# A fused two-block transformer kernel: GpSimd subtracts the low parts of nine down-projection weight tiles in each FFN of block 2

## The chip, the cores and the metric

The kernel runs on one core of a Trainium2 chip. The metric is the device time of one launch in microseconds (us), the median of several launches. Beside it stands one profiled execution, from which all durations below are read.

The engines are named as the profile names them: PE (TensorE, matrix multiply), PEld (its weight load), DVE (VectorE), ACT (ScalarE), POOL (GpSimd), SP (SyncE, which here only issues DMAs). SBUF is the on-chip memory that all of them read, PSUM the accumulators that PE writes.

## The reference, cut to what matters

The reference applies two transformer blocks to 256 tokens of width 1024, each block with two layers. The change touches the feed-forward part of block 2, `conv_ffn`, in both layers:

```
u = x @ w_up                                  # 1024 -> 5632
u = causal depthwise convolution of 3 taps over the tokens, plus bias
a, g = split(u, 2)                            # 2816 each
f = (a * silu(g)) @ w_down                    # 2816 -> 1024
x = layer_norm(DEEPNORM_ALPHA * x + f)
```

Everything is float32.

## The kernel before, in words

**Split weights.** PE multiplies in a rounded format (float32r). To keep float32 accuracy each weight tile is held in two parts. ACT copies the loaded tile `raw` into `whi` (rounded), line 1335. DVE then forms the remainder `wlo = raw - whi`, line 1714, one TENSOR_TENSOR with both operands in SBUF. PE multiplies with both parts. A tile is 128 partitions by 2048 elements (1 MB). "hi(t)" and "lo(t)" below are these two steps for tile t, and "the split" of a tile on DVE is lo(t).

**Order of the tiles.** `plan_tiles` writes out the order in which PE uses them. The FFN of a layer has 11 steps (FS = 11). Step s uses g_s (gate half of w_up, 256 features), u_s (up half), and then one tile of w_down: d_{s-1} for s = 1 to 5, none in step 6, d_{s-2} for s = 7 to 10. After step 10 come d_9 and d_10 together. So there are 33 tiles to each FFN.

**Buffers.** `raw` and `wlo` are rings of five tiles, `whi` is a ring of three. One more set (`xraw`, `ext`) holds g_0 of an FFN, and the first tile of the next layer's w_in. hi(t) can be made once PE is done with the tile three places earlier (`hi_room`). `serve(key)`, on ACT and on DVE, makes every split whose room comes free with tile `key`; both engines make all splits in the same written order (`split_order`). Each engine runs its instructions strictly in program order.

**One step s of the FFN of block 2.**
- PE: 32 matmuls for g_s, 32 for u_s (`by_features_wide`, lines 809 to 813) and 24 for the down tile (`down`, lines 737 to 739). It waits for lo of the tile (`take`), for the sums of the step before, and for `hid_ready` of the hidden slice that the down tile multiplies.
- ACT: copies the low half of the gate sums out of PSUM (L1397), runs the convolution's middle tap (L1686), hi(g_{s+1}) (L1335), silu (L1693). Then the same for the up half: L1397, L1686, hi(u_{s+1}), and last the hi of the next down tile, d_s in steps 1 to 4 and d_{s-1} in steps 7 to 9.
- DVE: adds the halves of the gate sums (L1877, one operand in PSUM), two more taps in four SCALAR_TENSOR_TENSORs (L2319), lo(g_{s+1}). Then L1877 and L2319 for the up half, the product (L2335), its rounded part (L2341), its remainder (L2343, which raises `hid_ready`), then lo(u_{s+1}), then lo of the same down tile as ACT.
- POOL: nothing. In block 2 it computes the reciprocal square roots of the norms (`norm_scale`, L2370), some copies (L2424, L2430) and the softmax division of the attention (L2382). Its next instruction in an FFN is the one for the norm behind it.

Down tiles 9 and 10 are split by DVE during step 10 and behind it. In step 9 of the first layer's FFN the split of the next layer's first w_in tile (into `ext`) stands ahead of lo(g_10).

Of the kernel before, what the change touches and what calls it, by code (L numbers as in the profile page):

```python
# [8 lines left out]
F32 = mybir.dt.float32  # L9
F32R = mybir.dt.float32r  # L10
I32 = mybir.dt.int32
ALU = mybir.AluOpType
# [8 lines left out]
L = 2  # L21
TC = 256
FF = 2816
FS = FF // TC
# [201 lines left out]
def build(nc, w, c, out):  # L226
    tiles, ti, geo = plan_tiles(w)
# [12 lines left out]
    split_order = []  # L240
    split_ring = [i for i in ring if i not in between.values()]
    split_seq = {i: q for q, i in enumerate(split_ring)}
    for i in halved:
        here = [e for e in extra if extra[e] == i]
        split_order += here + [i] if here and tiles[here[0]][0][1] == "in" else [i] + here
    rank = {i: q for q, i in enumerate(split_order)}
    load_order = []
    for i in order:
        load_order += [e for e in extra if extra[e] == i and tiles[e][0][1] == "in"]
# [26 lines left out]
    def unit0(block, l):  # L276
        return next(u for u, x in enumerate(units) if x[0] == block and x[1] == l)

    with ExitStack() as ctx:
# [3 lines left out]
        def sem(name):  # L283
            return ctx.enter_context(nc.semaphore(name))
# [77 lines left out]
        mem_ready = sem("mem_ready")  # L362
        hi_ready = sem("hi_ready")
        lo_ready = sem("lo_ready")
        tile_done = sem("tile_done")
        ident_loaded = sem("ident_loaded")
        angles_loaded = sem("angles_loaded")
# [159 lines left out]
        def tile_flat(buf, i):  # L527
            ap = tiles[i][1]
            return place(buf, i)[:, 0:ap.shape[1] * ap.shape[2]]

        def tile_view(buf, i):
            return tile_flat(buf, i).rearrange("p (k c) -> p k c", k=tiles[i][1].shape[1])
# [18 lines left out]
        def bc(ap, n):  # L551

            return ap.unsqueeze(1).broadcast_to([P, n, ap.shape[1]])
# [175 lines left out]
        def _(pe):  # L729
            def take(key):  # L730

                pe.wait_ge(lo_ready, rank[ti[key]] + 1)
                return tile_view("hi", ti[key]), tile_view("lo", ti[key])

            def product(o, lh, ll, rh, rl, first, last):
# [16 lines left out]
            def token_stage(block, name, l, n, ready, head, tail, free=lambda g, t: None, before={}):  # L752

                for q, t in passes(n, head, tail):
                    if (q, t) in before:
                        before[(q, t)]()
                    key = (block, name, l, q)
                    g, k0, whole = geo[key]
                    wh, wl = take(key)
                    kt, cols = wh.shape[1], wh.shape[2]  # L760
                    if k0 == 0:
                        free(g, t)
                    tok = slice(t * P, (t + 1) * P)
                    for kk in range(kt):
                        k = k0 + kk
                        turns_ready(ready, t, k)
                        ins = product(token_bank(g, t)[:, 0:cols], xhi[:, k, tok], xlo[:, k, tok], wh[:, kk, :],
                                      wl[:, kk, :], k == 0, k == KD - 1)
                    if t == 1:
                        ins.then_inc(tile_done, 1)  # L770
                    elif whole:
                        ins.then_inc(part_done, 1)

            def latent_products(key, outs, ah, al):

                wh, wl = take(key)
                kt = wh.shape[1]
                for t in range(NT):
                    for k in range(kt):
                        tok = slice(t * P, (t + 1) * P)  # L780
                        ins = product(outs[t], ah[:, k, tok], al[:, k, tok], wh[:, k, :], wl[:, k, :],
                                      k == 0, k == kt - 1)
                ins.then_inc(tile_done, 1)
# [327 lines left out]
            for l in range(L):  # L1111
# [78 lines left out]
                for i in range(2):  # L1190
                    pe.wait_ge(cmp_x, 2 * l + i + 1)
                    key = (2, "w1", l, i)
# [514 lines left out]
        def _(dve):  # L1707
# [2 lines left out]

            def split(i):

                dve.wait_ge(hi_ready, rank[i] + 1)
                v.tensor_tensor(tile_flat("lo", i), tile_flat("raw", i), tile_flat("hi", i).bitcast(F32),  # L1714
                                ALU.subtract).then_inc(lo_ready, 1)
# [643 lines left out]
        @block.gpsimd  # L2359
        def _(pool):  # L2360
            g = nc.gpsimd

            scaled = [0]

            def norm_scale(token_tiles=range(NT)):

                for t in token_tiles:
                    scaled[0] += 1
                    pool.wait_ge(ln_var, scaled[0])
                    g.tensor_tensor(rstd[:, t:t + 1], vare[:, t:t + 1], mhalf[:, t:t + 1],  # L2370
                                    ALU.pow).then_inc(ln_rstd, 1)

            def attention(block, l):
                first = 2 * unit0(block, l)
                count = 2 * sum(1 for x in units if x[0] == block and x[1] == l)
                for i in range(first, first + count):
                    u, hf = divmod(i, 2)
                    nk = (units[u][3] + 1) * P
                    x = soft[:, u % 2].rearrange("p (a q) k -> p a q k", a=2)[:, :, 2 * hf:2 * hf + 2, 0:nk]
                    rd = rden[:, u % 2, :].rearrange("p (a q) -> p a q", a=2)[:, :, 2 * hf:2 * hf + 2]  # L2380
                    pool.wait_ge(rden_ready, i + 1)
                    g.tensor_tensor(x, x, rd.unsqueeze(3).broadcast_to([P, 2, 2, nk]),  # L2382
                                    ALU.mult).then_inc(prob_ready, 1)

            pool.wait_ge(mhalf_ready, 1)
            norm_scale()
            norm_scale()
            pool.wait_ge(tables_ready, 1)
            for l in range(L):
                pool.wait_ge(ki_var, l + 1)  # L2390
                g.tensor_tensor(rstd[:, 0:NT], vare[:, 0:NT], mhalf[:, 0:NT], ALU.pow).then_inc(ki_rstd, 1)

                t1 = pt[:, 1:3, :].rearrange("p a b -> p (a b)")[:, 0:640].rearrange("p (h d) -> p h d", h=10)
                t2 = pt[:, 2:4, :].rearrange("p a b -> p (a b)")[:, 384:1024].rearrange("p (h d) -> p h d", h=10)
                x = proj1[:, 0, QA:QA + 640].rearrange("p (h d) -> p h d", h=10)
                for h0, h1 in ((0, H), (H, H + 2)):

                    pool.wait_ge(proj_ready, 8 * l + (5 if h0 == 0 else 7))
                    n, hs = h1 - h0, slice(h0, h1)
                    g.tensor_tensor(t1[:, hs], x[:, hs], bc(cos64[:, 0, :], n), ALU.mult)  # L2400
                    g.tensor_tensor(t2[:, hs, 0:32], x[:, hs, 32:64], bc(sin64[:, 0, 0:32], n), ALU.mult)
                    g.tensor_tensor(t2[:, hs, 32:64], x[:, hs, 0:32], bc(sin64[:, 0, 32:64], n), ALU.mult)
                    pool.drain()
                    if h0 == 0:
                        g.tensor_tensor(roped[:, 0, 0:4 * P].rearrange("p (r a d) -> p a r d", a=2, d=DH),
                                        t1[:, 0:8, :].rearrange("p (a r) d -> p a r d", a=2),
                                        t2[:, 0:8, :].rearrange("p (a r) d -> p a r d", a=2), ALU.add)
                    else:
                        g.tensor_tensor(roped[:, 0, 4 * P:5 * P].rearrange("p (h d) -> p h d", h=2),
                                        t1[:, 8:10, :], t2[:, 8:10, :], ALU.add).then_inc(qka_roped[0], 1)  # L2410
                attention(1, l)
                norm_scale()

                for t in range(NT):
                    for _ in range(2 if l == L - 1 else 1):
                        norm_scale([t])

            for l in range(L):
                pool.wait_ge(c_var, l + 1)
                g.tensor_tensor(rstdc[:], varc[:], mhalf[:], ALU.pow).then_inc(c_rstd, 1)  # L2420

                pool.wait_ge(proj2_ready, 8 * l + 6)
                for t in range(NT):
                    ins = g.tensor_copy(nqp[:, t, :].rearrange("p (r g d) -> p g r d", r=4, g=2),  # L2424
                                        proj2[:, t, NQ:NQ + 512].rearrange("p (g r d) -> p g r d", g=2, r=4))
                ins.then_inc(kd_ready, 1)

                pool.wait_ge(proj2_ready, 8 * l + 6)
                for e in range(2):
                    ins = g.tensor_copy(kdup[:, :, :, e, :],  # L2430
                                        proj2[:, :, KC:KC + 256].rearrange("p t (q d) -> p t q d", q=4))
                ins.then_inc(kd_ready, 1)
                attention(2, l)
                for _ in range(3):
                    norm_scale()


_NAMES = [
# [26 lines left out]
```

## Time and profile before

| | us |
|---|---|
| median of 3 launches | 1569.63 (1567.81 to 1573.33) |
| the profiled execution's own time | 1568.68 |
| its span | 1566.4 |
| PE busy | 1503.0 (96%) |
| DVE busy | 1072.9 (68%) |
| ACT busy | 765.3 (49%) |
| POOL busy | 122.9 (8%) |

The mean granted TensorE clock was 0.986 of full speed. PE is busy nearly all the time; what an edit beside it can change is the idle time between its matmuls. The chain of waits, which follows the last instruction back to what released it at each step, is 75% PE and 14% DVE. The FFN of the first layer of block 2 lies at about 940 to 1127 us of the span, that of the second at about 1373 to 1557 us.

### The profile page before, as it was taken

To read this page: it belongs to the slowest core of one execution; us is meant where nothing else is said; L and a number is where in the kernel's file an instruction comes from. 1 tells how busy PE (TensorE), PEld (TensorE's weight loads), DVE (VectorE), ACT (ScalarE), POOL (GpSimd) and SP (SyncE) were. 2 spreads that over 40 slices of the span, in tenths; PEclk is the share of its full clock that TensorE was granted. 3 is DMA by queue.
4 is the path that set the end of the run, shared out by engine and by line. 5 is a ranking of instruction groups with operands and counts; after the bars stand their busy time and mean duration, and the time that the engine had idled before them with its cause. 6 is when DMAs were issued, how large, how long until landed. Compare 5 with 4: busy or idle time off the path is not lost.

```text
span 1566.4 us, 21696 instructions
## 1 busy us (share of the span) xinstructions
PE 1503.0 (96%) x8429; PEld 1271.9 (81%) x8429; DVE 1072.9 (68%) x1735; ACT 765.3 (49%) x1136; POOL 122.9 (8%) x98
## 2 busy tenths in 40 slices
PE   8989999999899999999999999999899999999997
PEld 5767888888777888878877988888788779888886
DVE  7777687667766786685346457878852555678887
ACT  4563544444554444424474335555445653456562
POOL 0130000001210000011031000000010320000000
PEclk9999999999999999999899999999998999999999
DMA  7533655655236655635425635556545147345551
GB/s 259 193 104 132 217 190 191 213 190 181 90 119 209 218 189 189 242 114 168 154 91 172 218 114 188 188 188 215 162 123 172 62 151 246 130 162 188 189 187 55
DMA packets 184140, 265.01 MB, mean 169 GB/s; under 512 B 7336, under 2 KB 139366, under 8 KB 183912
## 3 DMA queue, kind: packets, MB, share of 16 engines
q1 hardware_dynamic: 178712, 258.38, 49.6%
q10 hardware_dynamic: 5328, 5.26, 1.0%
q8 instruction: 67, 1.10, 0.3%
q14 instruction: 33, 0.27, 0.1%
HBM read 258.38 MB, written 5.24 MB: 168 GB/s over the span
## 4 chain that ended last, share of the span: by engine, by line
PE 75%; DVE 14%; ACT 4%; issue 3%; DVEq 2%; POOL 1%; ACTq 0%; DMA 0%; POOLq 0%; SPq 0%
PE psw L810 16%; PE psw L737 7%; PE psw L739 7%; PE psw L738 7%; PE psw L809 7%; DVE wlo L1714 5%; PE psa L737 4%; PE psa L739 4%; PE psa L738 4%; PE psa L869 3%; PE psa L871 3%; PE psa L918 2%; PE psw L893 2%; PE psw L1196 1%; DVE r L2319 1%
## 5 line engine op out<-in xcount | busy, mean ns | idle before, releaser
L1714 DVE TENSOR_TENSOR wlo<-raw,whi 128x2048 fp32r<-128x2048 f32 (+3 forms) x199 | 448.5, 2264 | 125.4 <-ACT whi L1335 125.0
L810 PE MATMUL psw<-xboth,whi 128*128 128x512 f32 x1344 | 465.3, 396 | 4.8 <-DVE wlo L1714 4.8
L1335 ACT ACTIVATE whi<-raw 128x2048 fp32r<-128x2048 f32 (+3 forms) x199 | 374.2, 1886 | 180.2 <-PE psw L739 91.4
L809 PE MATMUL psw<-xboth,wlo 128*128 128x256 f32 x1176 | 327.9, 279 | 0.0
L810 PEld LDWEIGHTS psw<-xboth,whi 128*128 128x128 f32 x1344 | 242.9, 188 | 53.2 <-DVE wlo L1714 6.4
L809 PEld LDWEIGHTS psw<-xboth,wlo 128*128 128x128 f32 x1176 | 221.7, 189 | 7.5
L737 PE MATMUL psw<-whi,xboth 128*128 128x512 f32 (+3 forms) x472 | 181.8, 385 | 6.4 <-DVE wlo L1714 5.3
L739 PE MATMUL psw<-whi,xboth 128*128 128x512 f32 (+3 forms) x472 | 178.8, 379 | 0.0
L738 PE MATMUL psw<-wlo,xboth 128*128 128x512 f32 (+3 forms) x472 | 178.7, 379 | 0.0
L1397 ACT ACTIVATE r<-psw 128x512 f32<-128x512 f32 x88 | 52.6, 598 | 193.3 <-PE psw L810 182.8
L737 PE MATMUL psa<-whi,rr 128*128 128x512 f32 x352 | 137.3, 390 | 3.1 <-DVE wlo L1714 3.1
L738 PE MATMUL psa<-wlo,rr 128*128 128x512 f32 x352 | 137.0, 389 | 0.0
L2370 POOL TENSOR_TENSOR rstd<-vare,mhalf 128x1 f32<-128x1 f32 x26 | 36.7, 1414 | 1101.5 <-DVE vare L1736 1092.8
L2319 DVE SCALAR_TENSOR_TENSOR r<-r,pcol 128x254 f32<-128x254 f32 (+1 forms) x176 | 77.3, 481 | 57.1 <-ACT r L1686 53.8
L737 PEld LDWEIGHTS psw<-whi,xboth 128*128 128x128 f32 x472 | 88.8, 188 | 23.5 <-DVE wlo L1714 6.3
L739 PEld LDWEIGHTS psw<-whi,xboth 128*128 128x128 f32 x472 | 88.7, 188 | 15.8
L738 PEld LDWEIGHTS psw<-wlo,xboth 128*128 128x128 f32 x472 | 88.8, 188 | 15.0 <-issue 0.2
L739 PE MATMUL psa<-whi,rr 128*128 128x512 f32 x256 | 99.6, 389 | 0.0
L1877 DVE TENSOR_TENSOR r<-psw,r 128x512 f32<-128x512 f32 x88 | 60.5, 688 | 52.5 <-ACT r L1397 52.4
L1686 ACT ACTIVATE r<-r,pcol 128x256 f32<-128x256 f32 x88 | 48.2, 594 | 77.2 <-DVE r L1877 77.2
L1439 ACT ACTIVATE sy<-sy,nmx 128x256 f32<-128x256 f32 (+1 forms) x160 | 70.5, 444 | 20.9 <-DVE nmx L1813 20.9
L2382 POOL TENSOR_TENSOR sy<-sy,rden 128x512 f32<-128x512 f32 (+1 forms) x40 | 62.8, 1570 | 217.4 <-DVE rden L1825 176.1
(287 smaller groups left out, 2218.6 us busy)
## 6 DMA issues: line engine op xcount, KB each, us to landing
raw<-in_w_gu SPq DMA_DIRECT2D x44, 1024.0 KB, 5.1
raw<-in_ffn_w_up SPq DMA_DIRECT2D x42, 1024.0 KB, 5.1
raw<-in_w_down SPq DMA_DIRECT2D x22, 1024.0 KB, 4.9
raw<-in_ffn_w_down SPq DMA_DIRECT2D x22, 1024.0 KB, 4.9
raw<-in_w_in SPq DMA_DIRECT2D x20, 1024.0 KB, 5.3
raw<-in_xa_wkv SPq DMA_DIRECT2D x16, 1024.0 KB, 5.4
raw<-in_w_o SPq DMA_DIRECT2D x8, 1024.0 KB, 5.2
raw<-in_w_out SPq DMA_DIRECT2D x8, 1024.0 KB, 5.1
```

What stands on the lines that cost most here:

```text
L737: pe.matmul(o, lh, rh, start=first, stop=False)
L738: pe.matmul(o, lh, rl, start=False, stop=False)
L739: return pe.matmul(o, ll, rh, start=False, stop=last)
L809: pe.matmul(bank[:, 0:S], wl[:, k, cols], xhi[:, k, :], start=False, stop=False)
L810: ins = pe.matmul(bank.rearrange("p (i s) -> p i s", i=2), wh[:, k, cols], xboth[:, :, k, :], start=k == 0, stop=k == KD - 1)
L1335: nc.scalar.activation(tile_flat("hi", i), tile_flat("raw", i), ACT.Copy).then_inc(hi_ready, 1)
L1397: nc.scalar.activation(low_part[:, i], psw[:, 2 * i:2 * i + 2, S:2 * S], ACT.Copy).then_inc(low_out, 1)
L1439: ins = nc.scalar.activation(soft[:, u % 2, h, 0:nk], soft[:, u % 2, h, 0:nk], ACT.Exp, bias=nmx[:, u % 2, h:h + 1], scale=1.0, accum_out= ...
L1714: v.tensor_tensor(tile_flat("lo", i), tile_flat("raw", i), tile_flat("hi", i).bitcast(F32), ALU.subtract).then_inc(lo_ready, 1)
L1877: v.tensor_tensor((gsum, usum)[i].rearrange("p (c s) -> p c s", c=2), psw[:, 2 * i:2 * i + 2, 0:S], low_part[:, i], ALU.add).then_inc(ffn_ ...
L2319: ins = v.scalar_tensor_tensor(out=o, in0=whole[:, ch * S:(ch + 1) * S - lag], scalar=pcol[:, 1 + 2 * l, cc:cc + 1], in1=o, op0=ALU.mult, ...
L2382: g.tensor_tensor(x, x, rd.unsqueeze(3).broadcast_to([P, 2, 2, nk]), ALU.mult).then_inc(prob_ready, 1)
```

## The change

Nine down tiles of each FFN of block 2 (d_0 to d_8, in both layers: 18 tiles) are no longer split by DVE. POOL makes their lo with the same subtraction. It waits for hi of the tile and counts on a semaphore of its own, `pool_lo_ready`; the counts of `lo_ready` close up. POOL's loop stands between the second and the third norm of the layer.

```diff
+    pool_tiles = [ti[(2, "d", l, j)] for l in range(L) for j in range(FS - 2)]
+    pool_rank = {i: q for q, i in enumerate(pool_tiles)}
+    low_rank = {i: q for q, i in enumerate(i for i in split_order if i not in pool_rank)}
...
+        pool_lo_ready = sem("pool_lo_ready")
...
             def take(key):
 
-                pe.wait_ge(lo_ready, rank[ti[key]] + 1)
+                if ti[key] in pool_rank:
+                    pe.wait_ge(pool_lo_ready, pool_rank[ti[key]] + 1)
+                else:
+                    pe.wait_ge(lo_ready, low_rank[ti[key]] + 1)
                 return tile_view("hi", ti[key]), tile_view("lo", ti[key])
...
             def split(i):
 
+                if i in pool_rank:
+                    return
                 dve.wait_ge(hi_ready, rank[i] + 1)
                 v.tensor_tensor(tile_flat("lo", i), tile_flat("raw", i), tile_flat("hi", i).bitcast(F32),
                                 ALU.subtract).then_inc(lo_ready, 1)
...
                 attention(2, l)
-                for _ in range(3):
+                for _ in range(2):
                     norm_scale()
+                for j in range(FS - 2):
+                    down = ti[(2, "d", l, j)]
+                    pool.wait_ge(hi_ready, rank[down] + 1)
+                    g.tensor_tensor(tile_flat("lo", down), tile_flat("raw", down), tile_flat("hi", down).bitcast(F32),
+                                    ALU.subtract).then_inc(pool_lo_ready, 1)
+                norm_scale()
```

## Rows read from the trace of the kernel before

**Rows 1.** Waits inside FFN 1: engine, line, releaser, us in total, times, longest.

```profile
PE psw L810 <- DVE wlo L1714: 2.8, 3, 1.4
PE psa L737 <- DVE wlo L1714: 2.1, 1, 2.1
```

**Rows 2.** The same view inside FFN 2.

```profile
PE psw L810 <- DVE wlo L1714: 2.0, 2, 1.4
PE psa L737 <- DVE wlo L1714: 1.0, 1, 1.0
```

**Rows 3.** DVE timeline, steps 1 and 2: start, us, engine, instruction, form, count.

```profile
964.70 0.68 DVE L1877 TENSOR_TENSOR r<-psw,r 128x512 f32<-128x512 f32 x1
970.39 4.49 DVE L1714 TENSOR_TENSOR wlo<-raw,whi 128x2048 fp32r<-128x2048 f32 x2
974.80 0.68 DVE L1877 TENSOR_TENSOR r<-psw,r 128x512 f32<-128x512 f32 x1
978.51 2.29 DVE L1714 TENSOR_TENSOR wlo<-raw,whi 128x2048 fp32r<-128x2048 f32 x1
990.82 0.68 DVE L1877 TENSOR_TENSOR r<-psw,r 128x512 f32<-128x512 f32 x1
```

**Rows 4.** ACT timeline: the end of step 1, then steps 4 and 5.

```profile
966.48 3.71 ACT L1335 ACTIVATE whi<-raw 128x2048 fp32r<-128x2048 f32 x2
1017.40 1.92 ACT L1335 ACTIVATE whi<-raw 128x2048 fp32r<-128x2048 f32 x1 [0.85 <-PE psa L739]
1022.92 0.60 ACT L1397 ACTIVATE r<-psw 128x512 f32<-128x512 f32 x1 [3.61 <-PE psw L810]
1039.55 0.60 ACT L1397 ACTIVATE r<-psw 128x512 f32<-128x512 f32 x1 [3.61 <-PE psw L810]
```

**Rows 5.** POOL timeline: two-operand sums and products of five sizes.

```profile
60.34 1.30 POOL L2405 TENSOR_TENSOR r<-pt 128x512 f32<-128x512 f32 x1
58.73 0.79 POOL L2401 TENSOR_TENSOR pt<-r,sin 128x256 f32<-128x256 f32 x1
65.16 0.46 POOL L2409 TENSOR_TENSOR r<-pt 128x128 f32<-128x128 f32 x1
819.16 1.90 POOL L2382 TENSOR_TENSOR sy<-sy,rden 128x1024 f32<-128x1024 f32 x1 [0.78 <-DVE rden L1829]
779.78 1.04 POOL L2382 TENSOR_TENSOR sy<-sy,rden 128x512 f32<-128x512 f32 x1 [45.28 <-DVE rden L1825]
```

**Rows 6.** POOL and DVE timelines, where both work in SBUF, attention of block 2.

```profile
823.30 2.28 DVE L1714 TENSOR_TENSOR wlo<-raw,whi 128x2048 fp32r<-128x2048 f32 x1
823.46 3.88 POOL L2382 TENSOR_TENSOR sy<-sy,rden 128x1024 f32<-128x1024 f32 x1 [2.40 <-DVE rden L1829]
826.57 2.91 DVE L1714 TENSOR_TENSOR wlo<-raw,whi 128x2048 fp32r<-128x2048 f32 x1 [0.99 <-ACT whi L1335]
```

**Rows 7.** ACT, POOL and DVE timelines in block 1, both layers, rotation of heads.

```profile
56.37 0.45 DVE L1780 TENSOR_TENSOR sy<-r,sin 128x288 f32<-128x288 f32 x1
387.33 0.60 ACT L1533 ACTIVATE r<-psw 128x512 f32<-128x512 f32 x1 [2.09 <-PE psw L739]
388.01 1.29 POOL L2400 TENSOR_TENSOR pt<-r,cos 128x512 f32<-128x512 f32 x1 [11.53 <-ACT r L1533]
388.04 1.87 DVE L1778 TENSOR_TENSOR sy<-r,cos 128x576 f32<-128x576 f32 x1
389.83 0.98 DVE L1779 TENSOR_TENSOR sy<-r,sin 128x288 f32<-128x288 f32 x1
390.46 0.96 POOL L2402 TENSOR_TENSOR pt<-r,sin 128x256 f32<-128x256 f32 x1
390.74 1.00 DVE L1780 TENSOR_TENSOR sy<-r,sin 128x288 f32<-128x288 f32 x1
```

**Rows 8.** The same two timelines, where DVE has an operand in PSUM.

```profile
816.32 0.68 DVE L1839 TENSOR_TENSOR xboth<-psa,xboth 128x512 fp32r<-128x512 f32 x1
816.49 1.90 POOL L2382 TENSOR_TENSOR sy<-sy,rden 128x1024 f32<-128x1024 f32 x1 [3.98 <-DVE rden L1829]
```

## The prediction

> **What bounds the kernel now.** I read the busy shares first (PE 96%), then the waits inside the two FFNs that the change touches, then the timelines of DVE, ACT and POOL there. The shares say that only PE's idle time is to be had. The waits show all of it that these splits cause: in FFN 1 PE waits for DVE's lo for 2.8 us before up tiles and 2.1 us before the last down tile [rows 1], in FFN 2 for 2.0 and 1.0 us [rows 2]. Together 7.9 us, 0.5% of the time: this is all that unloading DVE can win.
>
> Where do these waits come from? One DVE step, from one gate sum to the next, takes 990.82 - 974.80 = 16.02 us when DVE is behind [rows 3]. PE's step takes 1039.55 - 1022.92 = 16.63 us when PE is ahead of nothing [rows 4]. So DVE is only 0.6 us a step faster. It is behind at two places: at the start of an FFN (until about u_2) and behind step 6, which has no down tile for PE, so that PE reaches u_8 early. At both, PE stands before an up tile. In FFN 1 a third place is u_10, because of the extra w_in split in step 9.
>
> **What the change removes from DVE.** A split occupies DVE for 2.20 us (two in a row take 4.41 until the next instruction starts: 974.80 - 970.39) [rows 3]. A step with a down tile falls to 13.8 us of DVE. If nothing else happened, DVE would no longer be late.
>
> **What it adds: POOL's duration.** No row shows POOL subtracting 2048 elements. Two contiguous operands took it 1.30 us for 512 and 0.46 us for 128 [rows 5]: 2.19 ns an element, so 1.30 + 1536 x 2.19 = 4.66 us. The other end: with a broadcast operand, 1.90 us for 1024 and 1.04 us for 512 [rows 5], 1.68 ns an element, which gives 3.62 us for 2048. I take 4.66, because the added instruction too has two contiguous operands; 3.62 stays as the lower bound. Upwards: 0.79 us for 256 against 0.46 for 128 [rows 5] is 2.58 ns an element, at most 0.46 + 1920 x 2.58 = 5.4 us. Between hi(d) and PE's use of d lie two other tiles of PE (11 us), so this length alone costs nothing.
>
> **What it costs: the two engines exclude each other.** This is the term that decides. At 823.46 POOL starts a product that takes 1.90 us elsewhere; it takes 3.88, and 0.16 us before it DVE had started a split of 2.28 us [rows 6]. POOL stood until DVE was through. It then holds DVE: the next split takes 2.91 instead of 2.28 us, 0.63 us late, so it began to work at 827.20, when POOL's instruction was 0.14 us from its end [rows 6]. It also goes the other way round with small ones: DVE's 288-element product takes 1.00 us beside POOL, 0.45 us alone [rows 7]. I read it as one resource, held for a whole instruction, by whichever came first. An instruction of DVE with an operand in PSUM isn't touched: 0.68 us, with POOL's at its usual 1.90 [rows 8]. So the sums (L1877) go on, and the products, L2335, the remainder L2343 and the splits stand. POOL's hold H is then about 4.66 - 0.16 = 4.5 us: more than twice the 2.20 us of DVE that it frees.
>
> The Trainium skill says the same in "SBUF — State Buffer", section "SBUF: two separate sides": DVE with two SBUF inputs and GpSimd share a port pair, taken exclusively for the whole instruction, not shared by bandwidth. The trace agrees (3.88 against 1.90 us). The skill's "GPSIMD Engine Reference", section 3.1, gives 4497 ns for a GpSimd tensor_tensor of 2048 float32; by it H would be 4.34 and the sum below 28.0 instead of 29.3 us. No row here shows that length.
>
> **Who comes first.** hi(u) and hi(d) stand back to back on ACT: they end at 966.48 + 3.71 = 970.19 [rows 4], and DVE starts the split of u at 970.39 [rows 3]. POOL starts 0.08 us behind an ACT result (387.33 + 0.60 = 387.93 to 388.01 [rows 7]), so at 970.27, 0.12 us ahead of DVE. At 388.01 POOL was ahead by 0.03 us and DVE waited [rows 7]; at 390.46 it queued behind a running DVE product and was let in before DVE's next one at 390.74 [rows 7]. So where DVE is behind, POOL takes the resource just before the split that PE is waiting for. In the steps where PE is on time, ACT must first wait for PE's down tile (the 0.85 us at 1017.40 [rows 4]); POOL then comes behind the split of u, and its 4.5 us fall for the most part into DVE's waits for PE and ACT: cost 0.
>
> **The sum**, place by place, H = 4.5:
> - Start of an FFN. d_0's hold falls on the product of step 0, before `hid_ready`: +H. Its split is gone from DVE: -2.20. d_1's hold falls before the split of u_2: +H. PE already waits for that split now (1.4 us, the longest wait of [rows 1]), so all of it counts: 2H - 2.2 = 6.8 us.
> - Behind step 6. The same with d_5 (product of step 6) and d_6 (before u_8), and PE already waits there: 6.8 us.
> - u_10 in FFN 1. From the end of g_9, DVE needs 0.70 us until the gate sum (copy on ACT and two hand-overs), 3.7 to the first split (978.51 - 974.80 [rows 3]), 2.2 for the w_in tile, 2.2 for g_10, 5.7 from the up sum to the split (970.39 - 964.70 [rows 3]), H, and 2.2 for u_10: 16.7 + H. PE has 16.6 us of work in that time. It waits H = 4.6 us instead of 0.7: +3.8. In FFN 2 there is no w_in tile, POOL comes behind u_10, 0.
> - The end of FFN 1. PE comes to d_10 that much later, while DVE has no d_8 to do: the wait of 2.1 us [rows 1] falls to about 0.4: -1.7. In FFN 2 it stays.
> - FFN 1: 6.8 + 6.8 + 3.8 - 1.7 = 15.7. FFN 2: 13.6. Together +29.3 us.
>
> The norm behind POOL's loop costs nothing: POOL is done with d_8 a step before it. ACT and the DMAs are only moved by PE's stalls. The profiled execution took 1568.68 us, so 1598.0; the median is 0.95 us above it, so I predict 1599 us. With the lower bound of POOL (H = 3.46) each pair costs 4.7: 18.9 + 2.8 - 1.7 = 20.0, or 1590. With 5.4 us of POOL (H = 5.25) it is 8.3 a pair: 33.2 + 4.6 - 1.7 = 36.1, or 1606. This forecast's own range is 1589 to 1607.
>
> **Rivals.**
> 1. DVE's split of u gets in first (the 0.12 us turns out the other way). For it: it is a small margin. Against: both cases of rows 7. Then d_1 and d_6 run behind the split and hold DVE's next taps instead, for the part that its waits don't cover (some 2.6 of 4.5 us, no more than the removed split). Left are d_0 and d_5: 2 x (H - 2.2) = 4.6 an FFN, and about 1 us for u_10 and the end: +11 us, 1581.
> 2. The other side, faster: no exclusion for this instruction (POOL reads two contiguous tiles, or the interlock passes them), so DVE is 2.2 us lighter in 18 steps and every wait for lo goes. It decides if the split beside a running POOL stays at 2.28 us. It wins 7.9 us less about 1 for d_0, whose POOL lo comes later than DVE's did: 1562. Against it: rows 6, with this very split.
> 3. The holds fall into idle time nearly everywhere (POOL shorter, and other phases once PE has stalled): within 0.3%, 1570. Against: DVE has 0.6 us a step to spare, and H is 4.5.
>
> **Chances.** Forecast 0.60, rival 1 0.22, rival 2 0.09, rival 3 0.09. 0.3% (4.7 us) is about what a measurement of this kernel can tell from no change. The forecast and rival 1 are slower by more than that: 0.82. Rival 2 gives 0.09 faster, rival 3 0.09 same. The range takes in rival 1, leaves out rivals 2 and most of 3, and ends where POOL takes 5.4 us, and one more: 1573 to 1607.
>
> **What would show it.** POOL's L1714-like subtraction of 128x2048 at 4.6 us alone and up to 6.8 where it queued behind a split. DVE splits of u_2 and u_8 with 6.7 instead of 2.28 us, and the product L2335 of steps 0 and 6 with 5 instead of 0.69 us. PE's waits before up tiles: 6 to 8 us at u_2 and u_8 in both FFNs, 4.6 at u_10 in FFN 1, now through DVE's wlo; no wait for POOL's lo worth naming. Steps 3 to 5 at 16.6 us. Block 1 and the attention unchanged. Wrong it is if the splits of u are at 2.28 us everywhere, or if PE's longest waits are for POOL.

## The result, and the profile of the changed kernel

The changed kernel takes 1611.2 us (median of 4 runs, 1607.2 to 1616.0) against 1569.1 us of the kernel before on the same chip: a ratio of 1.0267, with a 95% interval of 1.0249 to 1.0285. It is 42 us slower, where 30 us were forecast, and lies 4 us above the top of the range. The profiled execution is the slowest of the four: 1616.02 us, with a span of 1613.8 us against 1566.4 us before (+47.4).

Group table of the page for the changed kernel (line, engine, operation, names and form, count, busy us, mean ns, idle before and its releaser). Against before, line numbers of PE and ACT have moved by 7, those of DVE by 9.

```profile
L1723 DVE TENSOR_TENSOR wlo<-raw,whi 128x2048 fp32r<-128x2048 f32 (+3 forms) x181 | 430.3, 2383 | 125.6 <-ACT whi L1342 125.2
L817 PE MATMUL psw<-xboth,whi 128*128 128x512 f32 x1344 | 475.3, 403 | 31.3 <-DVE wlo L1723 31.3
L2448 POOL TENSOR_TENSOR wlo<-raw,whi 128x2048 fp32r<-128x2048 f32 x18 | 93.3, 5181 | 277.9 <-ACT whi L1342 277.9
```

DVE has lost 18 splits, and each remaining one takes longer on average (2383 ns; before it was 2264 ns). PE's idle time ahead of the up products is 31.3 us, where it was 4.8 us. PE's busy time has grown too, from 1503.0 to 1524.9 us, though it has the same 8429 products. The forecast had nothing for that.

POOL timeline in FFN 1: start, us, the instruction, and in brackets the idle time before it. All nine of the new instructions:

```profile
961.47 4.61 POOL L2448 TENSOR_TENSOR wlo<-raw,whi 128x2048 fp32r<-128x2048 f32 x1 [21.45 <-ACT whi L1342]
979.29 4.58 POOL L2448 TENSOR_TENSOR wlo<-raw,whi 128x2048 fp32r<-128x2048 f32 x1 [13.22 <-ACT whi L1342]
1001.97 5.58 POOL L2448 TENSOR_TENSOR wlo<-raw,whi 128x2048 fp32r<-128x2048 f32 x1 [18.10 <-ACT whi L1342]
1018.60 5.92 POOL L2448 TENSOR_TENSOR wlo<-raw,whi 128x2048 fp32r<-128x2048 f32 x1 [11.05 <-ACT whi L1342]
1035.22 5.92 POOL L2448 TENSOR_TENSOR wlo<-raw,whi 128x2048 fp32r<-128x2048 f32 x1 [10.71 <-ACT whi L1342]
1065.69 4.61 POOL L2448 TENSOR_TENSOR wlo<-raw,whi 128x2048 fp32r<-128x2048 f32 x1 [24.55 <-ACT whi L1342]
1083.51 4.58 POOL L2448 TENSOR_TENSOR wlo<-raw,whi 128x2048 fp32r<-128x2048 f32 x1 [13.21 <-ACT whi L1342]
1105.37 5.57 POOL L2448 TENSOR_TENSOR wlo<-raw,whi 128x2048 fp32r<-128x2048 f32 x1 [17.28 <-ACT whi L1342]
1123.22 4.62 POOL L2448 TENSOR_TENSOR wlo<-raw,whi 128x2048 fp32r<-128x2048 f32 x1 [12.29 <-ACT whi L1342]
```

The five of 4.6 us got in first (d_0, d_1, d_5, d_6, d_8); the four longer ones queued behind a DVE split. DVE timeline of the same FFN, the instructions that these two kinds met:

```profile
961.52 5.10 DVE L2344 TENSOR_TENSOR r<-r 128x512 f32<-128x512 f32 x1
979.43 6.59 DVE L1723 TENSOR_TENSOR wlo<-raw,whi 128x2048 fp32r<-128x2048 f32 x1
1000.78 2.28 DVE L1723 TENSOR_TENSOR wlo<-raw,whi 128x2048 fp32r<-128x2048 f32 x1
1006.14 0.69 DVE L1886 TENSOR_TENSOR r<-psw,r 128x512 f32<-128x512 f32 x1 [3.07 <-ACT r L1404]
1065.75 5.10 DVE L2344 TENSOR_TENSOR r<-r 128x512 f32<-128x512 f32 x1
1083.64 6.59 DVE L1723 TENSOR_TENSOR wlo<-raw,whi 128x2048 fp32r<-128x2048 f32 x1
1123.35 6.64 DVE L1723 TENSOR_TENSOR wlo<-raw,whi 128x2048 fp32r<-128x2048 f32 x1
```

POOL starts at 979.29 and DVE 0.14 us later at 979.43. Its split, 2.29 us in [rows 3], takes 6.59. At 1001.97 it is the other way round: POOL waits out the split of 1000.78, and its hold falls into the 3.07 us in which DVE waits for ACT anyway.

PE's waits inside FFN 1 and inside FFN 2 (as [rows 1] and [rows 2]), one fence for each:

```profile
PE psw L817 <- DVE wlo L1723: 17.9, 5, 6.3
PE psa L744 <- DVE rr L2352: 0.8, 1, 0.8
PE psa L744 <- DVE wlo L1723: 0.6, 1, 0.6
```

```profile
PE psw L817 <- DVE wlo L1723: 13.4, 4, 6.3
PE psa L744 <- DVE wlo L1723: 1.0, 1, 1.0
PE psa L744 <- DVE rr L2352: 0.9, 1, 0.9
```

FFN 1: 19.3 us against 4.9 before. FFN 2: 15.3 against 3.0. Together +26.7 us; the forecast had +29.3. So the waits are nearly as forecast, and still 20.7 of the 47.4 us of span are missing.

The first product of FFN 1 starts at 948.02, before the change at 941.18, and up to there the two kernels run the same instructions: 6.8 of the 47.4 us aren't the change's. From its first product to the first one behind it FFN 1 is longer by 21.4 us, the stretch between the FFNs by 3.1, and the rest, from the first product of FFN 2 on, by 16.1. By how much the two FFNs grew beyond their waits, 21.4 + 16.1 - 26.7 = 10.8 us, is what has to be explained.

It shows in a view that the forecast didn't use there, the windows: for each stretch its length, the busy time of PE, PEld, DVE, ACT and POOL, the granted TensorE clock, the DMA share and GB/s. The changed kernel, behind the three long waits of FFN 1:

```profile
980.00:985.00 5.00, 0.00 (x0) 0.00 (x0) 5.00 (x1) 0.37 (x1) 3.87 (x1) 0.97 0.56 210
985.00:990.00 5.00, 3.93 (x12) 3.43 (x13) 3.70 (x7) 3.19 (x4) 0.00 (x0) 0.50 0.00 0
1085.00:1090.00 5.00, 0.00 (x0) 0.00 (x0) 5.00 (x1) 0.00 (x0) 3.09 (x1) 0.71 0.96 347
1090.00:1095.00 5.00, 4.71 (x17) 4.11 (x18) 3.71 (x7) 3.52 (x4) 0.00 (x0) 0.61 0.19 73
1125.00:1130.00 5.00, 0.49 (x3) 0.17 (x1) 5.00 (x2) 0.60 (x1) 2.84 (x1) 0.81 0.65 202
1130.00:1135.00 5.00, 4.96 (x16) 4.28 (x17) 3.70 (x6) 3.52 (x4) 0.00 (x0) 0.51 0.04 11
```

The kernel before, one slice of the same view, in step 2 of FFN 1:

```profile
985.00:990.00 5.00, 5.00 (x31) 4.37 (x30) 4.85 (x5) 1.53 (x2) 0.00 (x0) 1.00 0.69 211
```

PE stands for a whole slice (980 to 985), and when it works again the granted clock is 0.50, the 1.2 GHz level instead of 2.4. In 985 to 990 PE is busy for 3.93 us with 12 products; before, a slice of these FFNs in which PE is busy throughout holds 23 or more. Before, all slices between 940 and 1125 and between 1380 and 1555 have 1.00.

The price can be estimated: PE's busy time in a slice times (1 - granted clock) is time lost by the clock, 3.93 x 0.50 = 2.0 us in this one. Summed over 5-us slices it is 7.1 us in FFN 1 and 5.0 us in FFN 2, 12.1 together, a mean of 2.4 for each of the five long waits. Waits and clock make 14.4 + 7.1 = 21.5 us in FFN 1, which became longer by 21.4, and 12.3 + 5.0 = 17.3 in FFN 2, less 1.5 for a low stretch at its very start that only before has (1372 to 1377): 15.8, for 16.1. So the estimate fits the length of both. (Low stretches at the very start of FFN 2 are counted outside, here and below.)

Outside the two FFNs the same sum is 27.1 us, where before it was 17.8: +9.3. Waits, clock inside, clock outside: 26.7 + 12.1 + 9.3 = 48.1 us, for 47.4 of span. Of the 9.3, 7.7 fall ahead of 940 us, where the two kernels are alike, and this was the slowest of four executions. In the nine kernels below the outside part lies between 17.4 and 24.2 us. So most of it belongs to the execution and not to the change; whether the change causes any of it is open.

### The profile page after: what moved, and what is told of

It reads as the page before. It is cut to its first block, busy times and chain, and to the rows that moved or that the text cites. A ratio compares the mean times of both kernels' runs of the same rounds, so it can differ in the third digit from the quotient of the medians.

```text
span 1613.8 us, 21696 instructions
## 1 busy us (share of the span) xinstructions
PE 1524.9 (94%) x8429; PEld 1287.4 (80%) x8429; DVE 1073.0 (66%) x1717; ACT 766.8 (48%) x1136; POOL 216.1 (13%) x116
## 4 chain that ended last, share of the span: by engine, by line
PE 72%; DVE 16%; ACT 5%; issue 3%; DVEq 2%; POOL 1%; ACTq 0%; POOLq 0%; DMA 0%; SPq 0%
PE psw L817 16%; PE psw L744 7%; PE psw L816 7%; PE psw L746 7%; PE psw L745 7%; DVE wlo L1723 6%; PE psa L744 4%; PE psa L746 4%; PE psa L745 4%; PE psa L876 3%; PE psa L878 3%; PE psw L900 2%; PE psa L925 2%; DVE r L2344 2%; DVE r L2328 2%
## 5 line engine op out<-in xcount | busy, mean ns | idle before, releaser
L1723 DVE TENSOR_TENSOR wlo<-raw,whi 128x2048 fp32r<-128x2048 f32 (+3 forms) x181 | 430.3, 2383 | 125.6 <-ACT whi L1342 125.2
L817 PE MATMUL psw<-xboth,whi 128*128 128x512 f32 x1344 | 475.3, 403 | 31.3 <-DVE wlo L1723 31.3
L816 PE MATMUL psw<-xboth,wlo 128*128 128x256 f32 x1176 | 332.2, 283 | 0.0
L817 PEld LDWEIGHTS psw<-xboth,whi 128*128 128x128 f32 x1344 | 248.1, 192 | 82.6 <-DVE wlo L1723 34.6
L816 PEld LDWEIGHTS psw<-xboth,wlo 128*128 128x128 f32 x1176 | 226.4, 192 | 7.8
L2448 POOL TENSOR_TENSOR wlo<-raw,whi 128x2048 fp32r<-128x2048 f32 x18 | 93.3, 5181 | 277.9 <-ACT whi L1342 277.9
```

Of the source, the lines that this page charges most:

```text
L816: pe.matmul(bank[:, 0:S], wl[:, k, cols], xhi[:, k, :], start=False, stop=False)
L817: ins = pe.matmul(bank.rearrange("p (i s) -> p i s", i=2), wh[:, k, cols], xboth[:, :, k, :], start=k == 0, stop=k == KD - 1)
L2448: g.tensor_tensor(tile_flat("lo", down), tile_flat("raw", down), tile_flat("hi", down).bitcast(F32), ALU.subtract).then_inc(pool_lo_ready, 1)
```

## The experiments

The theory is the forecast's (the waits come from GpSimd holding a resource ahead of DVE, where DVE is late), with the clock as a second term; the rivals stand in each expectation. All ratios are to the kernel before on the same chip, with 95% intervals.

**1. GpSimd later (e1_late).** The subtraction waits until DVE has made the hidden part of its step and the low part of the up tile.

```diff
                     pool.wait_ge(hi_ready, rank[down] + 1)
+                    step = j if j < LAG_STEP - 1 else j + 1
+                    pool.wait_ge(hid_ready, FS * (L + l) + step + 1)
+                    pool.wait_ge(lo_ready, low_rank[ti[(2, "u", l, step + 1)]] + 1)
```

> The changed kernel, but POOL waits before each of its nine subtractions for the remainder of the hidden slice and for DVE's split of the next up tile, the two instructions that stood in front of the removed split on DVE. POOL's work is the same 4.6 us with the same operands; only its place moves behind the split that PE waits for. Theory 1 (what costs is that POOL holds DVE just before u_2, u_8 and u_10): DVE's splits of u tiles are back at 2.28 us, PE's waits before up tiles fall from 31 us to under 8, the long low-clock stretches behind them go, and the time is 1570 to 1582. Rival (POOL's 4.6 us are too much wherever they stand, since H is twice what it frees): each of the places where DVE is behind still loses 2.3 us, and more DVE taps are held; 1590 or above.

Measured: 1577.1 us, ratio 1.0050 (1.0029 to 1.0072). The same 18 instructions, in another place, cost 7 us instead of 42. Its group line, and the two waits that took over:

```profile
L2451 POOL TENSOR_TENSOR wlo<-raw,whi 128x2048 fp32r<-128x2048 f32 x18 | 83.3, 4628 | 263.7 <-DVE wlo L1723 168.7 <-DVE rr L2352 95.1
PE psa L744 <- DVE wlo L1723: 5.0, 2, 2.6
PE psa L744 <- POOL wlo L2451: 4.9, 4, 1.3
```

All 18 are now at 4.6 us (mean 4628 ns): nothing is in their way. The price is new: PE now waits for GpSimd's low parts of d_0 and d_5 in both FFNs, and longer for DVE's low part of the last down tile (5.0 against 3.1 us). So the place decides, not the work.

**2. PE kept busy (e2_filler).** 24 products into a free PSUM bank stand ahead of the up tiles u_2 and u_8; PE runs them where it would wait. They are extra work whose result is dropped.

```diff
+                        if block == 2 and s in (2, 8):
+                            up_free(2)
+                            for _ in range(24):
+                                pe.matmul(psw[:, 2, :].rearrange("p (i s) -> p i s", i=2), xhi[:, 0, 0:P],
+                                          xboth[:, :, 0, :], start=True, stop=True)
```

> The changed kernel, plus 24 products of static data (5.4 us of PE work) into the free up bank just before PE waits for u_2 and u_8 in each FFN; the real product overwrites them. They lie inside the 6.3 us waits that the trace shows there. Theory 1 (what the time is above the forecast comes from TensorE's granted clock, which falls to 0.5 of full speed behind each 6 us wait; worked out from 5 us stretches, these four cost 15 us): the low stretches behind u_2 and u_8 go, the one behind u_10 of FFN 1 stays, DVE's and POOL's rows are unchanged, and the time falls to about 1597. Rival (the lower clock is the run's, not the wait's): the low stretches stay and the time stays at 1607 to 1616, or grows.

Measured: 1600.2 us, ratio 1.0196 (1.0164 to 1.0228): 11 us faster than the changed kernel, with more work. Windows at the same two places as above:

```profile
980.00:985.00 5.00, 4.03 (x21) 3.12 (x20) 3.90 (x2) 1.00 (x3) 1.15 (x1) 1.00 0.24 100
985.00:990.00 5.00, 5.00 (x30) 4.30 (x29) 4.15 (x6) 3.13 (x4) 0.00 (x0) 1.00 0.00 0
1090.00:1095.00 5.00, 5.00 (x26) 4.14 (x24) 3.03 (x6) 3.08 (x4) 0.00 (x0) 1.00 0.53 179
```

The low part that PE needs comes no earlier (the split of u_2 takes 6.69 us, GpSimd's 18 instructions have a mean of 5202 ns), but the clock stays at 1.00. The time lost by the clock in both FFNs falls from 12.1 to 2.3 us (what is left is at u_10, which has no filler). Of the 12.2 us by which the profiled span is shorter than the changed kernel's, 2.8 lie ahead of FFN 1; the other 9.4 go with these 9.7 us of clock, and show the clock as the missing term. The expectation had put the low stretches behind u_2 and u_8 at 15 us; by the slices they were 9.5.

**3. Shorter holds (e3_pieces).** The subtraction in four pieces of 512 elements.

```diff
-                    g.tensor_tensor(tile_flat("lo", down), tile_flat("raw", down), tile_flat("hi", down).bitcast(F32),
-                                    ALU.subtract).then_inc(pool_lo_ready, 1)
+                    for c in range(0, 2048, 512):
+                        ins = g.tensor_tensor(tile_flat("lo", down)[:, c:c + 512], tile_flat("raw", down)[:, c:c + 512],
+                                              tile_flat("hi", down)[:, c:c + 512].bitcast(F32), ALU.subtract)
+                    ins.then_inc(pool_lo_ready, 1)
```

> The changed kernel, but each of POOL's subtractions is cut into four of 512 elements. Theory 1 (the resource is held for one instruction and then goes to whoever waits): DVE gets in between the pieces, no DVE instruction is held longer than 1.3 us, PE's waits at u_2 and u_8 fall from 6.3 to about 3 us, and the time is about 1575 to 1585. Rival (POOL keeps it over its queue, or DVE's delay is set by POOL's total): the split of u_2 still takes 6 us or more and the time stays at 1600 or above.

Measured: 1581.2 us, ratio 1.0074 (1.0045 to 1.0103). At the split of u_2, POOL timeline and then DVE timeline:

```profile
974.24 7.35 POOL L2449 TENSOR_TENSOR wlo<-raw,whi 128x512 fp32r<-128x512 f32 x4 [10.26 <-ACT whi L1342]
974.37 3.38 DVE L1723 TENSOR_TENSOR wlo<-raw,whi 128x2048 fp32r<-128x2048 f32 x1
```

POOL is first here too, but DVE waits for one piece (3.38 - 2.28 = 1.1 us) instead of the whole 4.3, and POOL's other three pieces wait for DVE. The resource is handed over between instructions: its unit is the instruction. DVE's taps behind the gate sum were held here too, 3.26 us for four that take 1.83 otherwise.

**4. The gain alone (e4_nosplit).** Nobody makes the low parts of the 18 tiles; GpSimd's loop is left out, and PE multiplies by the high part a second time in their place.

```diff
-                    pe.wait_ge(pool_lo_ready, pool_rank[ti[key]] + 1)
-                else:
-                    pe.wait_ge(lo_ready, low_rank[ti[key]] + 1)
+                    pe.wait_ge(hi_ready, rank[ti[key]] + 1)
+                    return tile_view("hi", ti[key]), tile_view("hi", ti[key])
+                pe.wait_ge(lo_ready, low_rank[ti[key]] + 1)
...
```

> The changed kernel without POOL's subtractions: nobody makes the low parts of the 18 tiles, and PE multiplies by the high part a second time in their place (same number and shape of products). It leaves out those low parts. It is the change with its gain alone. Theory 1: waits for DVE's splits go nearly all, 7 us or so below before: 1559 to 1564. Rival (unloading DVE also changes something else, ACT's order or the clock, that costs): 1567 or above.

Measured: 1563.2 us, ratio 0.9950 (0.9931 to 0.9969). So taking the 18 splits off DVE for nothing is worth 7 us; the forecast read at most 7.9 us from [rows 1, 2].

**5 and 6. Which tiles (e5_near, e6_far).** GpSimd makes only d_0, d_1, d_5, d_6, or only d_2, d_3, d_4, d_7. The list stands in `pool_tiles` and in POOL's loop:

```diff
-    pool_tiles = [ti[(2, "d", l, j)] for l in range(L) for j in range(FS - 2)]
+    pool_tiles = [ti[(2, "d", l, j)] for l in range(L) for j in (0, 1, 5, 6)]
```

> GpSimd makes the low parts of d_0, d_1, d_5 and d_6 alone (the four tiles of each FFN whose subtraction fell ahead of a DVE instruction that PE was waiting for); DVE makes those of d_2, d_3, d_4, d_7 and, in FFN 1 and 2, d_8 as before. Theory A (the holds cost where DVE is behind, and they are bound to these four tiles): nearly all of the loss stays, PE waits about 6 us before u_2 and u_8 in both FFNs, some 25 us of stalls more than before, and with the clock behind them 1600 to 1611 us. Rival B (the loss comes from the sheer number of subtractions on GpSimd): 8 of 18, so 8/18 of the 42 us, 1588 us.

> GpSimd makes the low parts of d_2, d_3, d_4 and d_7 alone, those that ran in DVE's idle stretches in the changed kernel; DVE makes the other five of each FFN. Theory A (cost bound to the tile): these holds are free and DVE is 2.2 us lighter four times, 1568 to 1571 us. Theory A' (cost bound to DVE being behind, whichever tile stands there): DVE still is behind at u_2 and u_8 with its own splits, so that the start of an FFN goes as before, and a hold that meets DVE before it has caught up costs up to 4.5 us: some 6 us of stalls an FFN, 1580 to 1585 us. Rival B (the number): 1588 us, as near.

Measured: e5_near 1602.9 us, ratio 1.0208 (1.0193 to 1.0223); e6_far 1584.8 us, ratio 1.0101 (1.0083 to 1.0119). The four near tiles bring 33 of the 42 us, where the mere number would give 8/18 of them (1588 us): that rival is excluded. But the far ones, which cost nothing in the changed kernel (their holds lay in idle time), cost 15 us by themselves. DVE and POOL timelines of e6_far, behind step 2:

```profile
971.63 4.48 DVE L1723 TENSOR_TENSOR wlo<-raw,whi 128x2048 fp32r<-128x2048 f32 x2
987.65 6.67 DVE L1723 TENSOR_TENSOR wlo<-raw,whi 128x2048 fp32r<-128x2048 f32 x1
987.51 4.66 POOL L2448 TENSOR_TENSOR wlo<-raw,whi 128x2048 fp32r<-128x2048 f32 x1 [53.10 <-ACT whi L1342]
1010.21 5.56 POOL L2448 TENSOR_TENSOR wlo<-raw,whi 128x2048 fp32r<-128x2048 f32 x1 [18.03 <-ACT whi L1342]
```

The splits of u_2 and d_1 take 4.48 us, as before, and DVE is still late one step on. There d_2's subtraction stands, 0.14 us ahead of the split of u_3, which takes 6.67. The PE stall that follows lets DVE get ahead, and from then on POOL comes second (5.56). The cost belongs to the state "DVE is late", not to a tile: in both kernels the hold that met DVE in it was paid.

**7. A PE wait by itself (e7_dvedelay).** GpSimd as before; three more subtractions on DVE ahead of the splits of u_2 and u_8.

```diff
+                    if s in (1, 7):
+                        m = memT[:].rearrange("p k s -> p (k s)")
+                        for _ in range(3):
+                            dve.drain()
+                            v.tensor_tensor(r3[:, 2048:4096], m, m, ALU.subtract)
```

> The kernel before, GpSimd left as it is; DVE alone does three more subtractions of 128x2048 (6.6 us, into a part of memory that nothing reads) ahead of the splits of u_2 and u_8 in both FFNs. It asks for the price of a PE wait by itself, without GpSimd and without the shared resource. If a wait costs its own length: 4 x about 6 us, 1594 to 1597 us. If the clock falls behind each wait and takes 3 to 4 us more: 1605 to 1612 us, with the granted clock at 0.5 to 0.6 in a 5-us slice behind each wait.

Measured: 1607.3 us, ratio 1.0242 (1.0229 to 1.0255). PE's waits in the whole run, and windows behind the one at u_2:

```profile
PE psw L810 <- DVE wlo L1714: 32.8, 5, 8.5
```

```profile
975.00:980.00 5.00, 0.13 (x1) 0.13 (x1) 4.92 (x4) 0.00 (x0) 0.00 (x0) 0.50 0.12 47
980.00:985.00 5.00, 5.00 (x19) 4.32 (x20) 3.70 (x5) 2.29 (x3) 0.00 (x0) 0.62 0.00 0
```

The waits grew by 28.0 us, the span by 39.7. The time lost by the clock inside the two FFNs is 11.7 us, and 28.0 + 11.7 = 39.7. No GpSimd instruction was added: the clock term comes with the wait, and needs no GpSimd. Waits as long as their own length alone would have given 1598 us.

**8. The hold by itself (e9_dummy).** DVE makes every low part; GpSimd makes a subtraction whose result nobody reads, at the same nine places.

```diff
+                for j in range(FS - 2):
+                    pool.wait_ge(hi_ready, rank[ti[(2, "d", l, j)]] + 1)
+                    m = memT[:].rearrange("p k s -> p (k s)")
+                    pool.drain()
+                    g.tensor_tensor(r3[:, 2048:4096], m, m, ALU.subtract)
```

> The kernel before, with DVE making every low part; GpSimd runs a subtraction of 128x2048 with the same two contiguous operands' shape at the same nine places of each FFN, into memory that nothing reads, so that nobody waits for its result. Theory (the cost is the hold of the resource that DVE shares, whatever the result is for): the hold of 4.5 us stands ahead of DVE's instructions and DVE isn't 2.2 us lighter, so a DVE step takes 16.0 + 4.5 = 20.5 us against PE's 16.6 for as long as DVE is behind, and it never catches up: up to 9 x 3.9 = 35 us of waits in each FFN, at least the 6.8 + 2.2 = 9 us of each of the four places: 1615 to 1645 us, slower than the changed kernel. Rival (the cost is that PE needs GpSimd's result or that the two engines' order changed): within 3 us of before, 1567 to 1573 us.

Measured: 1635.6 us, ratio 1.0417 (1.0384 to 1.0450). Nothing waits for POOL here, and nothing that PE needs has changed its maker or order. DVE and POOL timelines:

```profile
976.92 7.91 DVE L1714 TENSOR_TENSOR wlo<-raw,whi 128x2048 fp32r<-128x2048 f32 x2
997.06 7.90 DVE L1714 TENSOR_TENSOR wlo<-raw,whi 128x2048 fp32r<-128x2048 f32 x2
1016.49 7.90 DVE L1714 TENSOR_TENSOR wlo<-raw,whi 128x2048 fp32r<-128x2048 f32 x2
976.88 3.60 POOL L2440 TENSOR_TENSOR r<-memT 128x2048 f32<-128x2048 f32 x1 [14.74 <-ACT whi L1335]
998.33 4.47 POOL L2440 TENSOR_TENSOR r<-memT 128x2048 f32<-128x2048 f32 x1 [17.85 <-ACT whi L1335]
```

The pair of splits takes 7.9 us instead of 4.49 [rows 3], step after step: with its own splits and the holds DVE is late again in step 4 (a PE wait of 3.9 us at u_4 in both FFNs), where in the changed kernel it had caught up; there the missing split pays part of it back. The rounding of the hidden slice (L2341, one operand in SBUF) is held too where it meets POOL: 3.67 us instead of 0.43. The hold is only 3.4 us here, since the instruction with twice the same operand takes 3.60 and not 4.6 us; so the 35 us of waits expected at most for an FFN weren't reached (18.9 + 4.9 = 23.8 us in FFN 1). PE's waits for low parts grew by 39.9 us in the whole run (47.8 against 7.9), the clock took 19.5 us in the two FFNs, and 6.4 us more than before outside. That is 65.8 of 69.1 us of span; the other 3.3 us are not placed.

**9. A better place for DVE's own split (e8_gap).** The kernel before, with DVE making a down tile's low part behind the next gate sum, where it waits for ACT's tap, instead of ahead of the sum.

```diff
-            def serve(key):
+            def serve(key, leave=False):
...
+                    if leave and tiles[split_order[nxt[0]]][0][1] == "d":
+                        return
...
+                        if s:
+                            serve(behind)
...
-                        serve((2, "u", l, s))
+                        serve((2, "u", l, s), s < FS - 1)
+                        behind = (2, "u", l, s)
...
-                            serve((2, "d", l, j))
+                            serve((2, "d", l, j), True)
+                            behind = (2, "d", l, j)
```

> The kernel before, GpSimd left as it is; DVE makes the low part of a down tile one place later: behind the next step's gate sum and ahead of its taps, where it waits 1.2 us for ACT, and so not ahead of the sum. Theory (only what DVE does between an ACT result and the up split is late, and DVE is 0.6 us a step ahead): about 1 us a step is won for DVE, the waits for lo before up tiles go (4.8 us in the two FFNs at most), 1564 to 1567 us. Rival: the split just moves the wait, the taps come 1 us later and with them ACT's gate, and nothing or up to 3 us is lost: 1569 to 1573 us.

Measured: 1565.2 us (median of 10), ratio 0.9976 (0.9964 to 0.9988): 4.5 us faster than before and 46 us faster than the changed kernel. DVE timeline and PE's wait before up tiles:

```profile
970.11 0.68 DVE L1879 TENSOR_TENSOR r<-psw,r 128x512 f32<-128x512 f32 x1
972.02 1.83 DVE L2321 SCALAR_TENSOR_TENSOR r<-r,pcol 128x255 f32<-128x255 f32 x4 [1.22 <-ACT r L1686]
978.76 0.69 DVE L1879 TENSOR_TENSOR r<-psw,r 128x512 f32<-128x512 f32 x1 [0.67 <-ACT r L1397]
979.37 2.28 DVE L1714 TENSOR_TENSOR wlo<-raw,whi 128x2048 fp32r<-128x2048 f32 x1
981.57 1.82 DVE L2321 SCALAR_TENSOR_TENSOR r<-r,pcol 128x255 f32<-128x255 f32 x4
PE psw L810 <- DVE wlo L1714: 1.0, 1, 1.0
```

Behind the up sum of step 1, where no split stands, the taps begin 1.2 us late, waiting for ACT (972.02); behind the gate sum of step 2 the down tile's split (979.37) fills that time, and DVE wins 1.2 us a step. PE's wait before up tiles falls from 4.8 to 1.0 us. The profiled execution was the slowest of the ten, with 5.7 us more of low clock outside the FFNs than before, so that its span (1566.5 us) doesn't show the gain; the medians do.

The spans of the profiled runs put together (us over the kernel before; the clock's part is PE's busy time times (1 - granted clock), over slices of 5 us; the waits are those of PE for DVE in the two FFNs, for e9_dummy for low parts in the whole run):

```
kernel       waits   clock in FFNs   clock outside   sum    span
after         26.7       12.1             9.3        48.1   47.4
e7_dvedelay   28.0       11.7             1.3        41.0   39.7
e9_dummy      39.9       19.5             6.4        65.8   69.1
```

## Why the prediction was wrong in size and right in mechanism

- **POOL's duration: right.** 4.66 us taken, 4.57 to 4.62 measured where it was first; up to 5.92 where it queued (up to 6.8 expected).
- **Who comes first: right.** POOL was ahead by 0.05 us (961.47 against 961.52) and 0.14 us (979.29 against 979.43), at the products of steps 0 and 6, at the splits of u_2 and u_8 in both FFNs, and at u_10. The hold was 5.10 - 0.69 = 4.4 us on the product and 6.59 - 2.29 = 4.3 us on the split; 4.5 was taken.
- **Start of FFN 1:** PE's waits grew by 5.9 us (6.33 + 0.84 + 0.16 - 1.42); 6.8 forecast. **Behind step 6:** 6.33 + 0.52 - 0.63 = 6.2; 6.8 forecast. The shorter hold is half or less of the difference, 4.4 + 4.3 - 2.2 = 6.5; the rest wasn't traced.
- **u_10:** 4.56 us, before it was 0.73: +3.8; 3.8 forecast. **End of FFN 1:** 0.6 against 2.1: -1.5; -1.7 forecast. **FFN 2:** +12.3; 13.6 forecast.
- **From waits to time: wrong, and this is the step that failed.** The sum took a microsecond of PE's wait as a microsecond of the run, and so put the granted clock's term at nothing without giving a reason. Behind each of the five waits of 4.6 to 6.3 us the granted clock stood at 0.50, and the products there ran at the 1.2 GHz level for some microseconds: 12.1 us in all. e7_dvedelay shows this without GpSimd, e2_filler takes it away while DVE's split comes as late as before. With that term the forecast would have been 1599 + 12 = 1611 us, which is the measured median. Part of this agreement is luck: the waits were forecast 2.6 us too high, and the median of before plus what was measured in the FFNs is 1569.1 + 26.7 + 12.1 = 1607.9 us; the other 3.3 us are not placed. The trace of before had a weak sign: behind PE's wait of 3.0 us at 408 to 411 the granted clock is 0.50 until 417. Its other low stretches stand behind waits of at most 1.4 us, and none lies inside these FFNs, where the longest wait was 2.1 us [rows 1], so that nothing in those rows told what a wait of six would cost.
- **The rivals.** DVE's split first: excluded by the 6.59 us at u_2 and u_8 in both FFNs. No exclusion: excluded by the same, and by experiment 3. Holds in idle time: true for four of nine tiles of FFN 1 in the changed kernel, and not a property of those tiles (e6_far).

The Trainium skill, "Perfetto Trace Analysis", section "Optimizing Scalar/DVE Operations", warns that moving work between these two engines might not help because they share an SBUF read port. The runs agree and go further: moved as here it costs 2.7%. On the clock, the Trainium skill's "TensorE: Matmul & The Clock Gate", section "Terms", reckons the penalty as the throttled time times the missing share of the clock. The 12.1 us are an estimate of this kind, with PE's busy time for the throttled time, and the trace agrees: by waits and clock FFN 1 would be 21.5 us longer, it is 21.4.

## What to carry to other kernels

Before work goes from VectorE to GpSimd, ask what VectorE is about to run when GpSimd's instruction becomes ready: in these runs, where both read SBUF, the whole GpSimd instruction stood ahead of it, 4.4 us for 2.2 us saved, and where VectorE was late TensorE paid for that. If it must be done, start it behind the critical VectorE instruction or cut it into pieces (42 us of loss became 7 and 11 here). And price a TensorE wait of several microseconds at more than its length: read the granted clock of the slices behind such waits.

## What the runs showed that was not expected

- From waits of 3.5 us on, the clock's part hardly grows with the length: 1.8 to 3.1 us behind the five waits of 4.6 to 6.3 us in the changed kernel, 2.1 to 3.0 behind the four of about 8 us in e7_dvedelay (the rest of its 11.7 is 1.3 behind a wait of 2.1), 1.4 to 2.8 behind four of 3.5 us in e6_far (8.3 in all).
- Behind shorter waits a low stretch sometimes came and sometimes not. Of the four waits of 2.4 us in e3_pieces two were followed by one (1.7 and 1.6 us). And one and the same wait for ACT, 3.0 us at about 78 to 81 us, was followed by none in the kernel before and by 2.8 us of it in the changed kernel, long ahead of the change. Slices behind it, the kernel before first:

```profile
80.00:85.00 5.00, 4.24 (x22) 3.62 (x24) 4.27 (x24) 2.36 (x12) 1.15 (x2) 1.00 0.08 26
80.00:85.00 5.00, 3.77 (x9) 3.05 (x10) 4.22 (x24) 2.36 (x13) 1.39 (x2) 0.52 0.08 26
```

- GpSimd's subtraction of 128x2048 takes 4.6 us with two different operands and 3.6 us with the same one twice.
- Unloading DVE by 2.2 us in 18 steps and moving one of its splits by one place in its order bring nearly the same (7 and 4.5 us): a good part of what could be had was in the order, not in the load.
